# A two-layer hybrid attention encoder on one core: other places for the side products, a second h buffer, high parts mixed first, and query weights on ScalarE's queue

## What is computed

```python
shift, scale, gate = split(silu(c) @ w_ada + b_ada, 3)
h = rms_norm(x, g_norm) * (1 + scale) + shift
q_lat, kv_lat, k_rope, z_a, q_b, k_b, v_b, z_b = split(h @ w_in)      # 256 128 32 512 512 128 128 512
# group A: 8 heads, queries and keys of 64 + 32 (rotary)
qa = rms_norm(q_lat, g_qa) @ w_uq;   k_nope, va = rms_norm(kv_lat, g_kva) @ w_ukv
ya = attention(qa, [k_nope, rotate(k_rope)], va) * silu(z_a)
# group B: 8 query heads on 2 key heads of 64, q and k normed and rotated
yb = attention(q_b, k_b, v_b) * silu(z_b)
x = x + gate * (concat(ya, yb) @ w_out)
```

## Time and profile before

| what | value |
|---|---|
| time, median of 3 runs (lowest to highest) | 2481.44 us (2475.5 to 2485.9) |
| profiled execution, its own time | 2479.77 us |
| its span in the profile | 2478.0 us |
| PE busy | 2064.9 us (83%) |
| DVE, ACT, POOL busy | 1395.4, 1020.7, 785.0 us |
| DMA moved | 293.90 MB |

### The profile page before, as it was taken

The page is one execution under the profiler, slowest core; times in us unless marked ns, Lnnn a source line. Parts: engine busy times, 40 slices in busy tenths (PEclk is TensorE's granted clock), DMA queues, the critical chain, the costliest instruction groups (busy, mean ns, idle before and its releaser), DMA issues.

```text
span 2478.0 us, 41818 instructions
## 1 busy us (share of the span) xinstructions
PE 2064.9 (83%) x14826; PEld 1123.5 (45%) x14826; DVE 1395.4 (56%) x2249; ACT 1020.7 (41%) x1994; POOL 785.0 (32%) x1208
## 2 busy tenths in 40 slices
PE   7587999678888899889837888868888999999986
PEld 1343444345444555455424444434444555555543
DVE  1445444334676766666633465543557676767763
ACT  0223433223455554555431344432335555565552
POOL 0255122144433312331202553313535331333120
PEclk9698999899999999999968889979989999999997
DMA  8544444513456654554582333242335555555553
GB/s 290 181 142 113 103 104 123 133 43 110 90 115 120 138 114 112 127 136 106 112 248 66 104 75 86 68 97 93 118 77 107 120 137 130 119 128 127 119 119 94
DMA packets 757962, 293.90 MB, mean 119 GB/s; under 512 B 703062, under 2 KB 727772, under 8 KB 757852
## 3 DMA queue, kind: packets, MB, share of 16 engines
q1 hardware_dynamic: 757856, 292.55, 47.9%
HBM read 112.04 MB, written 12.63 MB: 50 GB/s over the span
## 4 chain that ended last, share of the span: by engine, by line
PE 43%; DVE 17%; issue 13%; DMA 10%; ACT 8%; SPq 6%; POOL 3%; DVEq 1%; ACTq 0%; POOLq 0%
PE psum L617 33%; DMA region<-region 6%; PE psum L793 6%; DVE nmax L1062 5%; DVE region L1071 3%; PE psum L810 3%; ACT region L1221 3%; SPq L546 3%; DVE hT L917 2%; ACT region L1226 2%; DMA region<-x_after_layer 2%; POOL region L1275 1%; SPq L551 1%; DMA region<-in_x_sample 1%; PE psum L611 1%
## 5 line engine op out<-in xcount | busy, mean ns | idle before, releaser
L617 PE MATMUL psum<-Wq,hT 128*128 128x512 f32 (+1 forms) x1536 | 650.3, 572 | 19.5 <-DVE hT L917 13.2
L1071 DVE TENSOR_TENSOR region<-region 128x1024 f16<-128x1024 f32 (+1 forms) x384 | 435.8, 1137 | 151.2 <-ACT region L1226 112.5
L1062 DVE TENSOR_REDUCE nmax<-psum 128x1 f32<-128x1024 f32 (+1 forms) x384 | 399.1, 1039 | 211.8 <-PE psum L793 211.7
L617 PEld LDWEIGHTS psum<-Wq,hT 128*128 128x128 f32 x1536 | 293.5, 200 | 299.8 <-issue 252.6
L1221 ACT ACTIVATE region<-psum,nmax,unscale_a 128x1024 f32<-128x1024 f32 (+1 forms) x192 | 202.5, 1055 | 505.6 <-DVE nmax L1064 505.6
L1221 ACT ACTIVATE region<-psum,nmax,unscale 128x1024 f32<-128x1024 f32 (+1 forms) x192 | 202.5, 1054 | 405.2 <-DVE nmax L1064 384.2
L1226 ACT ACTIVATE region<-region 128x1024 f16<-128x1024 f32 (+1 forms) x384 | 351.2, 915 | 37.5 <-DMA region<-region 2.2
L617 PE MATMUL psum<-Wout,region 128*128 128x512 f32 x768 | 361.0, 617 | 5.7 <-DVE region L968 4.8
L1293 POOL TENSOR_TENSOR rinv<-stat,eps 128x1 f32<-128x1 f32 (+2 forms) x120 | 35.2, 294 | 901.6 <-ACT region L1137 869.5
L1275 POOL TENSOR_TENSOR region<-region,rope_sb 128x64 f32<-128x64 f32 (+3 forms) x384 | 195.6, 530 | 287.3 <-DVE region L1028 265.5
L810 PE MATMUL psum<-Vb,region 128*128 128x64 f16 x3840 | 158.2, 202 | 150.7 <-DMA region<-region 150.6
(11 more groups left out here) (128 smaller groups left out, 2009.5 us busy)
## 6 DMA issues: line engine op xcount, KB each, us to landing
Wout<-in_w_out SPq DMA_DIRECT2D x8, 2048.0 KB, 12.0
Va<-in_w_ada SPq DMA_DIRECT2D x12, 1024.0 KB, 5.8
Wq<-in_w_in SPq DMA_DIRECT2D x6, 2048.0 KB, 11.3
region<-region SPq DMA_TRANSPOSE x768, 2.8
xn<-x_after_layer SPq DMA_DIRECT2D x24, 512.0 KB, 3.4
Wq<-in_w_ada SPq DMA_DIRECT2D x5, 2048.0 KB, 13.4
xn<-in_x_sample SPq DMA_DIRECT2D x16, 512.0 KB, 3.7
x_after_layer<-region SPq DMA_DIRECT2D x12, 512.0 KB, 3.2
```

The lines of the kernel that those rows point to most:

```text
L617: last = nc.tensor.matmul(out, lhsTs[k], rhss[k], start=k == 0, stop=k == n - 1)
L1062: then(nc.vector.reduce_max(nmax[:, n:n + 1], scores_buf(h, S), AX_X, negate=True))
L1071: nc.vector.tensor_tensor(probs16_buf(h, S, 1), probs_buf(h, S), probs16_buf(h, S, 0), ALU.subtract).then_inc(s["probs_low"], 1)
```

## The change

- **Slots.** In the inner tiles `out0/1` goes from slot 3 to 4, `h^T1` to the front of slot 4, `q_lat` to the end of slot 5, `q_b/0` to slot 6, `q_r^T` ahead of `mix` of slot 11, `z_a/0` from behind `mix` of slot 13 to ahead of that of slot 12, and `y_a^T` behind it. `ada1` goes from slot 7 to behind `q_up0` of slot 8. The last tile has its own table for the output products. In the first tile of an instance `z_b/0` (and `ada0`) come before the second pair's scores.
- **Key phase.** `kv` comes after `kv^T` and the turns of the next h, and h has two buffers; ACT and GpSimd handle the next x tile at `h^T1`, ahead of their work on `kv`. The drain's rounds change their order.
- **Mix.** All products with the high part come first, and the wait for the low part's transpose stands behind them.
- **Maxima.** DVE's second instruction a head goes away; ACT makes the scaled maximum by a Copy with a scale, waits for it, and then starts the exponential.
- **Weights.** For both layers ACT issues the query weights, in three portions, in key steps 0, 1 and 2 of the prompt, after it has scaled the next x tile; SP issues none of them.

```diff
...
 GATE_B = {0: "z_b/0 |", 1: "z_b/1 |"}
-FINISH = {1: "y_b^T |", 2: "out0/0 |", 3: "out0/1 |", 9: "| out1/0", 10: "out1/1 |"}
-PREPARE = {2: "| h^T0", 3: "| h^T1", 4: "q_lat |", 5: "| q_b/0", 6: "q_b/1 |", 7: "q_lat^T |", 8: "q_up0 |",
-           9: "q_up1 |", 11: "| q_r^T", 13: "| z_a/0", 14: "z_a/1 |", 15: "q_b^T |"}
-TURN = {12: "y_a^T |"}
+FINISH = {1: "y_b^T |", 2: "out0/0 |", 4: "out0/1 |", 9: "| out1/0", 10: "out1/1 |"}
+FINISH_LAST = {1: "y_b^T |", 2: "out0/0 |", 5: "out0/1 |", 8: "out1/0 |", 11: "out1/1 |"}
+PREPARE = {2: "| h^T0", 4: "h^T1 |", 5: "| q_lat", 6: "q_b/0 |", 7: "q_b/1 q_lat^T |", 8: "q_up0 |",
+           9: "q_up1 |", 11: "q_r^T |", 12: "z_a/0 |", 14: "z_a/1 |", 15: "q_b^T |"}
+TURN = {12: "| y_a^T"}
...
 LEFT_OVER = {4: "| q_b^T@0"}
-ADA = {0: "ada0 |", 7: "ada1 |", 11: "| ada2"}
-KEY_ROUNDS = [("k^T", -2, 2), ("kv", 0, 5), ("kv^T", -1, 6), ("h^T0", 1, 0), ("h^T1", 1, 1),
+ADA = {0: "ada0 |", 8: "ada1 |", 11: "| ada2"}
+KEY_ROUNDS = [("k^T", -2, 2), ("kv^T", -1, 6), ("h^T0", 1, 0), ("h^T1", 1, 1), ("kv", 0, 5),
               ("kv_up0", -1, 7), ("kv_up1", -1, 6)]
...
 DRAIN_ROUNDS = [
-    [("k^T", -2, 2), ("q_lat", None, 5), ("kv^T", -1, 6), ("q_b", None, 0), ("kv_up0", -1, 7), ("kv_up1", -1, 6)],
-    [("k^T", -1, 2), ("q_lat^T", None, 5), ("q_up0", None, 0), ("q_up1", None, 7), ("z_a", None, 4), ("q_r^T", None, 1)]]
+    [("k^T", -2, 2), ("kv^T", -1, 6), ("q_lat", None, 5), ("kv_up0", -1, 7), ("kv_up1", -1, 6), ("q_b", None, 0)],
+    [("q_lat^T", None, 5), ("q_up0", None, 0), ("q_up1", None, 7), ("k^T", -1, 2), ("z_a", None, 4), ("q_r^T", None, 1)]]
...
 def slots(first, last, ada):
-    parts = ([ADA] if ada else []) + [LEFT_OVER if first else FINISH, GATE_B, TURN]
+    parts = ([ADA] if ada else []) + [LEFT_OVER if first else FINISH_LAST if last else FINISH, GATE_B, TURN]
     if not last:
-        parts.append(PREPARE)
+        parts.insert(0, PREPARE)
     return [[[n for p in parts for n in p.get(slot, "|").split("|")[a].split()] for a in (0, 1)]
             for slot in range(2 * HEADS)]
...
+        hTs = [hT[:, :, :], probs16[0].rearrange("p a n -> p (a n)").bitcast(F32).rearrange("p (k n) -> p k n", k=KD)]
...
+        WEIGHT_STEPS = [0, 1, 2]
...
+        def query_weights(queue, l, part):
+            w_in_l = w_in[l].rearrange("(k p) n -> p k n", p=P)
+            if part == 1:
+                for k in range(QR // P):
+                    w = w_uq[l][k * P:(k + 1) * P, :].rearrange("p (h d) -> p h d", h=HEADS)
+                    queue.dma_start(Wuq[:, k, 0:MIX].rearrange("p (h d) -> p h d", h=HEADS), w[:, :, 0:NOPE]) \
+                        .then_inc(s["wuq_loaded"], 16)
+                    queue.dma_start(Wuq[:, k, MIX:].rearrange("p (h d) -> p h d", h=HEADS), w[:, :, NOPE:QK]) \
+                        .then_inc(s["wuq_loaded"], 16)
+            for d0, c0, w in (((0, 0, QR), (Q_QB, C_ZA + MIX, MIX)), ((Q_ZA, C_ZA, MIX),), ((Q_ZB, C_ZB, MIX),))[part]:
+                queue.dma_start(Wq[:, :, d0:d0 + w], w_in_l[:, :, c0:c0 + w]).then_inc(s[f"wq_loaded{part}"], 16)
...
-                if l and r == 0:
-                    query_weights(l)
...
-                if q == 0:
-                    query_weights(0, (0,))
...
-                if q == 0:
-                    query_weights(0, (1,))
...
-                if q == 0:
-                    query_weights(0, (2,))
...
-                    h_done = at.get("h^T1", head_done) if isinstance(i, int) and i < 3 else step_start - 2
+                    h_done = at.get("h^T1", head_done) if isinstance(i, int) and i < 3 else step_start - 3
                     k_done = step_start
                     if not isinstance(i, int) or i > 2:
-                        k_done -= 5 if isinstance(i, int) and i == NT + 1 else 6
+                        k_done -= 6
...
                         if name in ("h^T0", "h^T1"):
+                            if name == "h^T0":
+                                pe.wait_ge(s["mm_free"], h_done)
...
-                            last = product(ps[:, 0:KVC], [hT[:, k, :] for k in range(KD)],
+                            last = product(ps[:, 0:KVC], [hTs[odd][:, k, :] for k in range(KD)],
...
-                            pe.wait_ge(s["mm_free"], k_done)
+                            pe.wait_ge(s["mm_free"], step_start if isinstance(i, int) and i > NT else k_done)
...
                     pe.wait_ge(s[f"high_turned{h % 2}"], turns(b0, i, h))
-                    pe.wait_ge(s[f"low_turned{h % 2}"], turns(b0, i, h))
-                    for c in range(NT):
-                        for a, b in ((0, 0), (0, 1), (1, 0)):
-                            v = Va[:, c, b, head, :] if head < HEADS else Vb[:, c, b, g * GD:(g + 1) * GD]
-                            last = nc.tensor.matmul(out, PT[h % 2][:, a, c, :], v, start=c == 0 and a + b == 0,
-                                                    stop=c == NT - 1 and a == 1)
+                    for a, parts in ((0, (0, 1)), (1, (0,))):
+                        if a == 1:
+                            pe.wait_ge(s[f"low_turned{h % 2}"], turns(b0, i, h))
+                        for c in range(NT):
+                            for b in parts:
+                                v = Va[:, c, b, head, :] if head < HEADS else Vb[:, c, b, g * GD:(g + 1) * GD]
+                                last = nc.tensor.matmul(out, PT[h % 2][:, a, c, :], v, start=c == 0 and a + b == 0,
+                                                        stop=c == NT - 1 and a == 1)
                     last.then_inc(s["pv_done"], 1)
...
+                        if first and h == 0:
+                            for name in before_mix:
+                                side(name, i)
                         if h % 2 == 0:
                             if h + 2 < 2 * HEADS:
                                 scores(h // 2 + 1, i)
                             elif not last:
                                 scores(0, i + 1)
-                        for name in before_mix:
-                            side(name, i)
+                        if h or not first:
+                            for name in before_mix:
+                                side(name, i)
...
-                    then(nc.vector.reduce_max(nmax[:, n:n + 1], scores_buf(h, S), AX_X, negate=True))
-                    by = unscale_a[:, m:m + 1] if h < HEADS else unscale[:, l:l + 1]
-                    nc.vector.tensor_scalar(nmax[:, n:n + 1], nmax[:, n:n + 1], by, None, ALU.mult).then_inc(s["max_ready"], 1)
+                    nc.vector.reduce_max(nmax[:, n:n + 1], scores_buf(h, S), AX_X, negate=True).then_inc(s["max_ready"], 1)
...
                             last.then_inc(s["kv_squared"], 1)
+                        elif name == "h^T1":
+                            x_square(2 * b0 + t + 1)
+                            x_scale(2 * b0 + t + 1)
+                            if r == 0 and isinstance(i, int) and i in WEIGHT_STEPS:
+                                act.wait_ge(s["mm_ready"], at[name])
+                                query_weights(nc.scalar, l, WEIGHT_STEPS.index(i))
...
-                    if not isinstance(i, int) or i < NT:
-                        x_square(2 * b0 + i + 2)
-                        x_scale(2 * b0 + i + 2)
...
-                    nc.scalar.activation(probs_buf(h, S), scores_buf(h, S), ACT.Exp, bias=nmax[:, n:n + 1], scale=scale,
+                    nc.scalar.activation(shift[:, n:n + 1], nmax[:, n:n + 1], ACT.Copy, scale=scale).then_inc(s["shift_ready"], 1)
+                    act.wait_ge(s["shift_ready"], heads(b0, i, h))
+                    nc.scalar.activation(probs_buf(h, S), scores_buf(h, S), ACT.Exp, bias=shift[:, n:n + 1], scale=scale,
                                          accum_out=sums[:, n:n + 1]).then_inc(s["exp_done"], 1)
...
                         n = at[name] = rounds.step()
+                        if name == "h^T1":
+                            x_rstd(2 * b0 + t + 1)
                         if name != "kv":
                             continue
                         row = kv_row[odd]
                         pool.wait_ge(s["kv_squared"], b0 + t + 1)
                         then(rstd(3, 3))
                         if not isinstance(t, int) or t > 0:
-                            pool.wait_ge(s["mm_ready"], n + 1)
+                            pool.wait_ge(s["mm_ready"], at["kv^T"])
...
                             .then_inc(s["k_ready"], 1)
-                        x_rstd(2 * b0 + t + 2)
...
```

41 lines of the change are left out of this document (15 added, 26 removed).

## The result

The changed kernel takes 2441.15 us (median of 4 runs, 2432.69 to 2443.96) against 2480.7 for the kernel before beside it: ratio 0.9835, 95% interval 0.9801 to 0.9868. It is faster, as forecast, but by 40 us instead of 122, and outside the range.

The account below looks back on a forecast made before the run. TensorE's order was taken as the bound, with its idle time and slow clock to be won: 2479.8 - 25 (weights) - 118 (tiles) + 21 (key phases) = 2358, by the median's distance 2359 us; range 2300 to 2425.

Parts of the forecast that it names:

- inner sample tiles: Twelve sample tiles, neither first nor last: `z_a/0` fills the waits at slots 12 and 13; net 6.0 us each, 72 together.
- thin stretch: Slots 10, 11 and 12, 13: PE has 6.9 us of work against 7.6 a pair, so waits 0.8 in each.
- start: Key phase beginning: first `kv` waits for the second h's turn; 8 us later per sample, 1 per prompt, together +18.
- drain: Key phase end: shorter wait ahead of `q_up0` (-3.2), less behind the last `kv` (-2.6); four times 5.8, -23 us.
- steps: Key phase steps: one wait of 2.9 us replaces 1.9, +1.0 a step (16), plus 10 for ACT's weight issue; +26.
- the clock in the key phase: Rival: a 2.9 us wait a step leaves `kv` at 7.45 instead of 5.85, total 2388 us; chance 0.10.
- First tiles: Four first tiles: `z_b/0` fills the 5.23 us wait ahead of the sample's second scores; 6.7 per sample, 2 per prompt, 17.
- the hole moved: Rival: PE waits as long ahead of the scores, an inner tile gains 2 us instead of 6, total 2419; chance 0.12.
- Last tile of layer 0's prompt: One of four last tiles, without `z_a`: about six waiting mixes gain 0.57 us each, taken as 3 a tile.
- the weights: Last sample tile of layer 0: the 31.25 us wait shrinks once SP no longer issues query weights; gain taken as 25.
- high parts first: In `mix`, two thirds (0.57 us) run before the low part lands; within the inner tiles' gain, 12 us in last tiles.
- The Copy: ACT's scaled maximum, twice in each pair's chain: taken as 0.3 us with its wait, bounds 0.2 and 0.6.

Follow-up runs that it names:

- b_store: Kernel before, with layer 1 also storing its finished rows right behind `out1` into a buffer nothing reads: 2498.83 us, ratio 1.0084.
- a_nonorm: Changed kernel without layer 1's final norm, rows stored behind `out1` as in layer 0: 2419.40 us, ratio 0.9776.
- a_late_f13_start: Changed kernel with `kv^T` in its own bank behind the h turns, final norm a slot later, each sample's first `kv` ahead of the second h: 2392.97 us.
- a_oldtables: Changed kernel with the side products in the slots of the kernel before, and the old order ahead of the first scores: 2494.71 us, ratio 1.0053.
- a_dveshift: Changed kernel with the scaled row maximum made by DVE's second instruction again, instead of ACT's Copy: 2454.45 us, ratio 0.9893.
- b_weights: Kernel before, with only the query weights moved to ScalarE's queue in the prompt's first key steps: 2468.12 us, ratio 0.9966.
- a_final13: Changed kernel with layer 1's final norm one slot later (`FINAL_SLOT` 13 instead of 12): 2438.63 us, ratio 0.9838.

## Why the forecast missed

**The step that failed: inner sample tiles.** One tile of layer 0 was taken for all twelve. For layer 0 the 6.0 us a tile is exact. (From the forecast's own numbers, 7.6 less 6.9, the wait in each thin stretch is 0.7 and not 0.8, which is 0.3 a tile.) Layer 1's hole was smaller (1.62 and 1.85) because no store stands between its transposes (b_store, 1.6 us a tile), so there was less to win; and with the hole filled, the final norm's square, hidden in it before, became what the next scores wait for (2.41; a_nonorm, 76.2). A window of one tile of layer 1 would have shown the first, its ACT rows the second. 28 of the 81 us missed: some 16 because layer 1's tiles were 79.6 and not 82.3 before, 12 by the final norm (78.25 against 76.2).

**Key phase: start and drain mis-sized.** By the three terms of the forecast, in both profiles (us, changed less before; prompt and sample of layer 0, then of layer 1):

| term | forecast | measured |
|---|---|---|
| start, to the second `kv` | +18 | +26.9 (3.4, 11.7, 1.1, 10.7) |
| steps, from there to the last `kv` | +26 | +27.6 (5.7, 7.4, 6.4, 8.1) |
| drain, from there to the first scores | -23 | -16.0 (-4.9, -2.9, -3.8, -4.4) |

*Start:* the first `kv` of layer 1's sample is 7.9 us late as forecast (7.3), but layer 0's is 13.4 late, and the second ones come 10.7 and 11.7 later, where I took 8. It is not the place of the first `kv` alone (a_late_f13_start): in the new order each `kv` stands behind the turns of one more x. In layer 1 the final norm of the prompt's last rows stands on ACT ahead of the second x, behind whose turns the first `kv` now comes; without it (a_nonorm) the second `kv` is only 2.7 late. *Steps:* the wait came where and as long as forecast (2.9; measured 2.6 to 3.1). A late step of a sample grew by 1.9 and not by 1.0, because `kv` took 5.75 to 7.45 us, at the lower clock for part of it, against 5.85: the rival called the clock in the key phase, which should have been in the sum. That the term as a whole came out is in part luck, since two steps of the kernel before were long themselves (13.87 and 11.50 in layer 1) and grew less. *Drain:* 4.18 to 0.90 is right, but behind the last `kv` stands the wait ahead of `kv^T` once more, 2.56 in both samples, which I had left out. Together 17 us missed.

**First tiles: the hole moved.** The 5.23 of the earlier trace rows is 2.00, but PE then waits at other places of the tile. In layer 0 all waits of 0.25 us or more come to 17.1 before and 17.1 after. In layer 1 they fall from 17.7 to 15.0, but the granted clock falls too (first row before, second after):

```profile
1819.14:1895.60 76.46, 60.25 (x566) 33.92 (x567) 57.27 (x70) 39.65 (x67) 38.48 (x31) 0.91 0.63 116
1784.90:1864.16 79.26, 63.88 (x567) 35.52 (x566) 52.96 (x54) 44.26 (x84) 40.56 (x32) 0.87 0.58 107
```

PE is busy for 3.6 us longer with the same work. With the old key phase before them both tiles take 75.6, at 0.93; whether the key phase sets this clock stays open, since the tile varies from run to run. 16 us.

**Last tile of layer 0's prompt:** forecast -3, measured +9.8; 13 us. I had costed that table only by its mixes. The tables cost it (a_oldtables); the cause within them stays open.

**Right:** the weights (25 forecast, 24 in the tile, 2.8 back in the key phase), the prompts' other tiles (-17.8 for -21), the last tiles (-4.6 for -6), `z_a/0` in the hole; high parts first were worth 20 us instead of the 12 of the last tiles. **The Copy** I charged at 0.3 twice a pair; the row of the group has 287 ns each:

```profile
L1225 ACT ACTIVATE shift<-nmax,unscale 128x1 f32<-128x1 f32 x192 | 55.2, 287 | 418.1 <-DVE nmax L1065 416.7
```

Its length was right, its place in the sum not: a_dveshift shows no cost in the inner sample tiles and a gain in the whole. On its length the estimate of 0.28 us worked out from the Trainium skill's page ScalarE: Activation LUTs (What ACT_TABLE_LOAD costs) agrees better than the row of 0.24.

On the weights, the Trainium skill's page DMA: Bandwidth & Descriptors (Issuing engines are not separate DMA queues) says that another issuer saves only its issue time. b_weights agrees, with 2.8 us more in the key phase, but what that issue time held up was a stall of 31.25 us.

## What to carry to other kernels

Before multiplying a gain read from one tile by the number of tiles, look at one tile of each kind: what differs (a store, a norm) is also what decides which wait comes next. When a wait is folded into another, look at what the wait is for: here a PSUM bank shared by two products made one product wait for the whole step before. The new key phase had lost 27 us; a bank of its own gave back 22, and a later place another 27. And what a late start costs is read at the second product, not only at the first. A product moved into a hole is worth the hole plus the slow clock behind it, and no more than the next engine's chain allows.

## What was unexpected

The same wait of 2.41 us, in tiles with the same instructions, was followed by scores at 1.46 us in one tile and at 0.82 in the next, with a granted clock of 0.98 and 1.00 over the tile; the tiles so come in two lengths, some 1.5 us apart. With the wait at 1.19 (a_final13) or 0.55 (a_nonorm) only one tile of twelve is longer and has the lower clock.
